# One-hot products for all 128 expert columns in one matmul each, placed beside the tiles of u

## What is computed

```python
q = (xb @ w_q).reshape(PEER_BLOCK, PEER_HEADS, 2, PEER_HALF)
scores = jnp.einsum('thpd,hpkd->thpk', q, sub_keys).astype(jnp.float32)
top_s, top_i = lax.top_k(scores, PEER_TOPK)
...
cand_i = (top_i[:, :, 0, :, None] * PEER_N_KEYS + top_i[:, :, 1, None, :]).reshape(...)
best_s, best_pos = lax.top_k(cand_s, PEER_TOPK)
expert = jnp.take_along_axis(cand_i, best_pos, axis=-1)
gate = jax.nn.softmax(best_s, axis=-1)
act = jax.nn.gelu(jnp.einsum('thkd,td->thk', u[expert], xb).astype(jnp.float32), approximate=False)
return jnp.einsum('thk,thkd->td', (gate * act).astype(v.dtype), v[expert])
```

## Time and profile before

| | us |
|---|---|
| median of 3 runs | 2359.57 (2357.17 to 2361.6) |
| the profiled execution, its own time | 2366.52 |
| its span, first to last instruction | 2365.1 |
| PE busy | 2232.4 (94%) |
| PEld busy | 1941.9 (82%) |
| DVE busy | 1621.3 (69%) |
| ACT busy | 1100.3 (47%) |
| POOL busy | 353.3 (15%) |
| share of the 16 DMA engines for loads | 44.8% |

### The profile page before, as it was taken

The page is one execution under the profiler, slowest core; times in us unless marked ns, Lnnn a source line. Parts: engine busy times, 40 slices in busy tenths (PEclk is TensorE's granted clock), DMA queues, the critical chain, the costliest instruction groups (busy, mean ns, idle before and its releaser), DMA issues.

```text
span 2365.1 us, 35299 instructions
## 1 busy us (share of the span) xinstructions
PE 2232.4 (94%) x14036; PEld 1941.9 (82%) x14036; DVE 1621.3 (69%) x2749; ACT 1100.3 (47%) x1671; POOL 353.3 (15%) x166
## 2 busy tenths in 40 slices
PE   8998979899999999799998878999999999999999
PEld 6887769888878887578887667999999998887887
DVE  5667793476666666866666765798466768897554
ACT  5554632155555555555555854444433333333443
POOL 0000102200010000100013112232222222222222
PEclk9998995799999999699999878999999999999999
DMA  5665130046545665146554224444544434443554
GB/s 193 189 191 173 61 134 11 1 153 190 190 162 178 189 189 171 45 136 191 189 198 161 80 81 160 164 163 159 182 148 150 144 127 147 149 146 128 187 194 153
DMA packets 96658, 352.15 MB, mean 149 GB/s; under 512 B 10880, under 2 KB 11776, under 8 KB 96048
## 3 DMA queue, kind: packets, MB, share of 16 engines
q1 hardware_dynamic: 96496, 349.90, 44.8%
HBM read 348.81 MB, written 1.05 MB: 148 GB/s over the span
## 4 chain that ended last, share of the span: by engine, by line
PE 80%; DVE 14%; ACT 3%; issue 1%; POOL 1%; DMA 0%; SPq 0%; ACTq 0%; DVEq 0%
PE psum L235 16%; PE psum L236 16%; PE psum L237 16%; PE psum L276 14%; PE psum L275 6%; PE psum L2494 4%; DVE tile_low L185 3%; PE psum L992 2%; ACT tile_high L173 1%; PE psum L279 1%; PE psum L318 1%; POOL small L1593 1%; DVE hT L468 1%; PE psum L756 1%; DVE peer_active L2696 1%
## 5 line engine op out<-in xcount | busy, mean ns | idle before, releaser
L173 ACT ACTIVATE tile_high<-raw_tiles 128x1024 fp32r<-128x1024 f32 x650 | 686.2, 1056 | 573.4 <-PE psum L237 573.1
L185 DVE TENSOR_TENSOR tile_low<-raw_tiles,tile_high 128x1024 fp32r<-128x1024 f32 x543 | 674.7, 1245 | 391.7 <-ACT tile_high L173 385.2
L276 PE MATMUL psum<-hT,tile_high 128*128 128x512 f32 x1408 | 495.2, 396 | 5.8 <-issue 5.2
L197 POOL TENSOR_TENSOR tile_low<-raw_tiles,tile_high 128x1024 fp32r<-128x1024 f32 x107 | 270.2, 2525 | 831.3 <-ACT tile_high L173 831.3
L235 PE MATMUL psum<-hT,tile_high 128*128 128x256 f32 x1280 | 372.5, 291 | 8.0 <-DVE tile_low L185 3.9
L235 PE MATMUL psum<-tile_high,hT 128*128 128x512 f32 (+1 forms) x848 | 346.4, 409 | 21.1 <-DVE mix_arena L2330 7.6
L236 PE MATMUL psum<-hT,tile_high 128*128 128x256 f32 x1280 | 365.5, 286 | 0.0
L237 PE MATMUL psum<-hT,tile_low 128*128 128x256 f32 x1280 | 365.3, 285 | 0.0
L275 PE MATMUL psum<-hT,tile_low 128*128 128x256 f32 x1232 | 344.3, 279 | 0.0
L236 PE MATMUL psum<-tile_low,hT 128*128 128x512 f32 (+1 forms) x848 | 335.8, 396 | 0.0
L237 PE MATMUL psum<-tile_high,hT 128*128 128x512 f32 (+1 forms) x848 | 335.4, 396 | 0.0
(11 more groups left out here) (332 smaller groups left out, 2790.8 us busy)
## 6 DMA issues: line engine op xcount, KB each, us to landing
raw_tiles<-ffn_in_dram SPq DMA_DIRECT2D x176, 512.0 KB, 3.8
raw_tiles<-peer_u_dram SPq DMA_DIRECT2D x128, 512.0 KB, 3.5
raw_tiles<-peer_v_dram SPq DMA_DIRECT2D x128, 512.0 KB, 3.5
raw_tiles<-ffn_out_dram SPq DMA_DIRECT2D x88, 512.0 KB, 3.5
raw_tiles<-w_kv_dram SPq DMA_DIRECT2D x16, 512.0 KB, 3.5
raw_tiles<-in_gates_dram SPq DMA_DIRECT2D x16, 512.0 KB, 3.5
raw_tiles<-peer_q_dram SPq DMA_DIRECT2D x16, 512.0 KB, 4.2
raw_tiles<-w_k_dram SPq DMA_DIRECT2D x8, 512.0 KB, 4.3
```

What stands on the lines that cost most here:

```text
L173: scalar.activation(k.high[:, n % SLOTS, :], k.raw[:, n % RAW_SLOTS, :], ACT.Copy).then_inc(*k.tile_high_made.mark(n))
L185: vector.tensor_tensor(k.low[:, n % SLOTS, :], k.raw[:, n % RAW_SLOTS, :], k.high[:, n % SLOTS, :].bitcast(F32), ALU.subtract).then_inc(*k ...
L197: pool.tensor_tensor(k.low[:, n % SLOTS, :], k.raw[:, n % RAW_SLOTS, :], k.high[:, n % SLOTS, :].bitcast(F32), ALU.subtract).then_inc(*k.p ...
L276: ins = k.tensor.matmul(ps, high[:, c, :], both[:, c, :, :], start=(c == 0), stop=(c == KC - 1), skip_group_check=True)
```

## The change

There is one side instead of two. `j_hot` and `j_gates` have all 128 columns, a lot's matmuls have 128 moving columns, and there are 64 lots in all. They stand after steps 68 to 131, beside tiles of u; none stand beside v.

When lot q is weighed (step 69 + q on VectorE), only the first `active_by(q)` columns of `active` exist: 52 for lot 0, 116 for lot 63. `weigh(q)` multiplies these in place. For the later columns the weights themselves are kept: `keep(q)`, new, on ScalarE one step later, copies them from PSUM to the place in `active` where the products will stand. When such a later column's tile is done, gelu is written in place into PSUM for the tokens whose weights wait (`waiting(g)` tokens) and into `active` for the rest, and `weigh_pair(g)`, new, on VectorE, multiplies the waiting weights by it. A lot's PSUM bank is emptied by `keep`, a pair's by `weigh_pair`.

At the turn from u to v, TensorE's sums in `hT` may be overwritten as soon as the last tile of u has passed those chunks (`chunks_passed`). At the end x takes in each of the four banks as soon as that bank is summed.

`j_hot` has a buffer of its own, single, and `hots(q)` waits for `hots(q - 1)`. The diff, cut to its core:

```diff
-FIRST_WEIGHED = len(range(0, 16)) + HALF + 1
+FIRST_WEIGHED = PICKS_AT + 2 * PICK_STEPS - 1
+def weighed_at(q):
+    return FIRST_WEIGHED + 3 + q
+def active_by(q):
+    return (weighed_at(q) - 2 * PH) // 2 * 2
+def waiting(g):
+    return LOT * sum(active_by(q) <= 2 * g for q in range(LOTS))
...
 # tensor_peer
-    def lot(side, q):
-        ps = bank(k, ("lot", side, q), k.weighed, (side, q))[:, 0:LOT * HALF].rearrange("p (j t) -> p j t", t=LOT)
+    def lot(q):
+        ps = bank(k, ("lot", q), k.weights_kept, q).rearrange("p (j t) -> p j t", t=LOT)
...
+    def chunks_passed(c, ins):
+        if c in (1, 3, 5):
+            ins.then_inc(*k.bank_summed.mark(("chunks", c // 2)))
...
-    while step < FIRST_WEIGHED + LOTS + 3:
-        beside(step)
-        step += 1
-    use_banks(k, range(4, 8))
...
-        if pair == HALF // 2:
-            while step < SECOND_WEIGHED + LOTS + 3:
-                beside(step)
-                step += 1
...
+                    if pair == PAIRS - 1 and i == 1 and (tb, half) != (1, 1):
+                        ins.then_inc(*k.bank_summed.mark(("peer", tb, half)))
             ins.then_inc(*k.tile_used.mark(n))
-            if pair < HALF // 2:
-                beside(step)
-                step += 1
...
 # scalar_peer
-            scalar.activation(r["active"][:, 2 * g:2 * g + 2, :], result(k, ("peer_u", g)).rearrange(
-                "p (j t) -> p j t", j=2), ACT.Gelu).then_inc(*k.activated.mark(g))
+            ps, n = result(k, ("peer_u", g)).rearrange("p (j t) -> p j t", j=2), waiting(g)
+            if n:
+                ins = scalar.activation(ps[:, :, 0:n], ps[:, :, 0:n], ACT.Gelu)
+            if n < T:
+                ins = scalar.activation(r["active"][:, 2 * g:2 * g + 2, n:T], ps[:, :, n:T], ACT.Gelu)
+            ins.then_inc(*k.activated.mark(("pair", g)))
+    def keep(q):
+        scalar.wait_ge(*k.weighed.at(q))
+        scalar.activation(r["active"][:, active_by(q):KEYS, lot_of(q)], result(k, ("lot", q)).rearrange(
+            "p (j t) -> p j t", t=LOT)[:, active_by(q):KEYS, :], ACT.Copy).then_inc(*k.weights_kept.mark(q))
...
     def part_high(pair):
         if pair >= 3:
             scalar.wait_ge(*k.tile_used.at(v + 2 * (pair - 3) + 1))
+        else:
+            scalar.wait_ge(*k.bank_summed.at(("chunks", pair)))
...
     for step in range(16 + KEYS):
+        if 0 <= step - 1 - weighed_at(0) < LOTS:
+            keep(step - 1 - weighed_at(0))
         if step and step % 2 == 0:
             out(step // 2 - 1)
         split_high(k, base + step + SLOTS)
         beside(step)
...
 # vector_peer
+        vector.tensor_tensor(j_hot, r["numbers"], across(r["j_of"](q), KEYS), ALU.is_equal).then_inc(*k.hot_steps.mark())
+        vector.tensor_tensor(i_hot, r["numbers"], across(r["i_of"](q), KEYS), ALU.is_equal).then_inc(*k.i_hot_made.mark(q))
         vector.wait_ge(*k.hot_steps.now())
+        vector.tensor_tensor(j_gates, j_hot.unsqueeze(1).to_broadcast([P, PARTS, KEYS, LOT]),
+                             r["gates_of"](q).unsqueeze(2).to_broadcast([P, PARTS, KEYS, LOT]), ALU.mult).then_inc(
+                                 *k.hot_made.mark(q))
...
+    def weigh_pair(g):
+        n = waiting(g)
+        if n:
+            a = r["active"][:, 2 * g:2 * g + 2, 0:n]
+            vector.wait_ge(*k.activated.at(("pair", g)))
+            vector.tensor_tensor(a, result(k, ("peer_u", g)).rearrange("p (j t) -> p j t", j=2)[:, :, 0:n], a,
+                                 ALU.mult).then_inc(*k.weighed.mark(("pair", g)))
...
+        if step % 2 == 0 and step >= 18:
+            weigh_pair(step // 2 - 9)
+        if 0 <= step - weighed_at(0) < LOTS:
+            weigh(step - weighed_at(0))
+        if 0 <= step - FIRST_WEIGHED - 1 < LOTS:
+            hots(step - FIRST_WEIGHED - 1)
...
-    vector.wait_ge(*k.tile_used.at(N_TILES - 1))
     for tb in range(TB):
         for half in range(2):
             xs = k.x[:, tb, half_of(half)]
-            vector.tensor_tensor(xs, k.psum[:, 2 * tb + half, :], xs, ALU.add).then_inc(*k.x_updated.mark(("peer", tb, half)))
+            vector.wait_ge(*(k.tile_used.at(N_TILES - 1) if (tb, half) == (1, 1) else k.bank_summed.at(("peer", tb, half))))
+            vector.tensor_tensor(xs, result(k, ("values", tb, half)), xs, ALU.add).then_inc(
+                *k.x_updated.mark(("peer", tb, half)))
```

More of the change, by code:

```diff
@@ L252, in half_of, with feature_major @@
     return slice(n * BANK, (n + 1) * BANK)
[L255 removed]
+def feature_major(k, ps, src, ready=None, passed=None):
     n, pair = take(k)
@@ L2517, in tensor_peer @@
             step += 1
-    for g in range(HALF):
-        ps = bank(k, ("peer_u", g), k.activated, g)
+    for g in range(PAIRS):
+        ps = bank(k, ("peer_u", g), k.weighed if waiting(g) else k.activated, ("pair", g))
         for i in range(2):
-            feature_major(k, ps[:, i * T:(i + 1) * T], k.hT)
+            feature_major(k, ps[:, i * T:(i + 1) * T], k.hT, passed=chunks_passed if (g, i) == (PAIRS - 1, 1) else None)
             beside(step)
             step += 1
-    while step < FIRST_WEIGHED + LOTS + 3:
-        beside(step)
-        step += 1
-    use_banks(k, range(4, 8))
[L2528 to L2531, removed]
-        if pair == HALF // 2:
-            while step < SECOND_WEIGHED + LOTS + 3:
-                beside(step)
-                step += 1
+    for tb in range(TB):
+        for half in range(2):
+            bank(k, ("values", tb, half), k.x_updated, ("peer", tb, half))
+    for pair in range(PAIRS):
         for i in range(2):
@@ L2607, in scalar_peer @@
         beside(step)
-    out(PH + HALF - 1)
-    step = 16 + KEYS
-    while step < FIRST_WEIGHED + LOTS + 3:
-        beside(step)
-        step += 1
-    part_high(0)
-    for pair in range(HALF):
-        if pair + 1 == HALF // 2:
-            while step < SECOND_WEIGHED + LOTS + 3:
-                beside(step)
-                step += 1
-        if pair + 1 < HALF:
+    part_high(0)
+    out(PH + PAIRS - 1)
+    for pair in range(PAIRS):
+        if pair + 1 < PAIRS:
             part_high(pair + 1)
@@ L2622, in scalar_peer @@
             split_high(k, v + 2 * pair + i + SLOTS)
-            if pair + 1 < HALF // 2:
-                beside(step)
-                step += 1
 def vector_peer(k):
@@ L2782, in vector_peer @@
         beside(step)
-    step = 16 + KEYS
-    while step < FIRST_WEIGHED + LOTS + 3:
-        beside(step)
-        step += 1
     part_low(0)
-    for pair in range(HALF):
-        if pair + 1 == HALF // 2:
-            while step < SECOND_WEIGHED + LOTS + 3:
-                beside(step)
-                step += 1
-        if pair + 1 < HALF:
+    weigh_pair(PAIRS - 1)
+    for pair in range(PAIRS):
+        if pair + 1 < PAIRS:
             part_low(pair + 1)
```

94 lines of the change are left out of this document (39 added, 55 removed).

## The result

| | before, us | after, us |
|---|---|---|
| median of 4 runs | 2360.6 (2357.2 to 2365.5) | 2332.0 (2329.2 to 2339.3) |
| the profiled execution's span | 2365.1 | 2328.5 |

The changed kernel takes 0.9883 of the time (95% interval 0.986 to 0.9906), 28.6 us less. 2294.5 was forecast, with a range of 2288 to 2318: the direction is right, the gain is less than half, and the time lies outside the range.

What follows compares the result with a forecast made beforehand. The prediction took TensorE to bound the expert stage; 3.2 + 0.6 − 6.5 − 61.0 − 2.6 − 1.8 + 3 = −65.1 us takes the profiled 2366.5 to 2301.4, a median of 2294.5, range 2288 to 2318.

Steps and rivals of the forecast that it cites:

- Part 1: Lots beside u: four more lots there cost +3.2 us, and doubling each lot's columns +0.6 us in all.
- The bound for added columns: Lots beside u: columns paid in full at 0.42 ns each, a lot of 1.11 us, +20 us in all.
- Rival C: Lots: operands four bf16 apart halve column reading; 111 ns a matmul, 1.36 us a lot, +36, 2331 us; chance 0.05.
- Rival A: Lots beside u: added columns cost time, 1.11 us a lot, 2314 us; chance 0.2.
- the 0.97 in its brackets: Lots: the Trainium skill's about 81 ns a matmul gives 0.97 us a lot, 2305 us.
- Rival D: Beside u: VectorE so late that TensorE stops every third tile, half clock follows; slower, 2379 us; chance 0.03.
- D's 4.1 us in three steps: Beside u: the time lost in three steps that gives +87 on 2291.5, 2379 us.
- Rival B: Beside u: VectorE becomes the bound, 0.3 us more a step than TensorE, +19 instead of +3, 2311 us; chance 0.2.
- Part 2: Turn from u to v: TensorE's 6.8 us gap shrinks to a wait of 0.3, −6.5 us.
- Part 3: V: all 128 tiles run as the second half did; −61.0 us in the first half, −2.6 in the second.
- Part 4: The end: three of four adds hide beside the next bank's matmuls, −1.8 us.
- Part 5: VectorE beside u: 9.8 to 11.1 us against TensorE's 11.0 in three steps; waits cost +3 us, bounds 0 and 19.

Runs made afterwards that it cites:

- the packed old form: Kernel before, its 128 narrow lots unmoved, each matmul's 64 moving and 64 output columns side by side; result not computed: 2322.4 us, 0.9837 of before.
- the token-by-token run: Changed kernel computing everything, j_hot, j_gates and PSUM bank laid out as (token, column), so moving and output columns are packed: 2362.8 us, 1.001 of before.
- the run with the turn undone: Changed kernel, but first three high parts wait for u's whole last tile and all four final adds for v's last: 672.1 us from last transposed pick against 668.9.

## Why the prediction was wrong

**Part 1 failed, and it alone made the miss.** The step that failed is its term for the 64 added columns: it said that a weight load sets the pace of a matmul, so that doubling the columns costs +0.6 us in all. It put a wide lot, with what it adds to a step, at 0.80 us; it takes 1.42. 64 × 0.62 is 39.7 us, so the term is 40 us and not 0.6; 2294.5 + 39.7 less the 3 us of waits that didn't come is 2331.2, and 2332.0 was measured. Two things in it were wrong:

- It took the f32 rows (L992 and L2476) as the nearest. They are near in having a weight load for each matmul, but they take 111 ns for 128 columns, twice as long as the columns themselves, so a stream at half rate would not show in them. The narrow lot was another case: it is held by its strided streams, and the packed old form shows 33 ns where the prediction saw a weight load of 63.
- The bound for added columns, 0.42 ns each, came from v's and u's matmuls, whose columns are packed in both streams. A bound must come from rows with the same access pattern; 64 more columns at half rate are 53 ns more a matmul, and 55 came.

**Rival C was the right one** for half of its reason, with a chance of 0.05: the step halves the rate at which columns are read. The output's step was in no rival, and C's narrow lots "at the pace of the weight load" are refuted by the 33 ns. That its price of 2331 is so near is partly luck: it took 111 ns from the f32 rows where 117 were measured, and kept 3 us of waits that didn't come. The numbers at hand could have spoken for C: 64 columns at half rate are 53 ns, and the row said 63. But a floor of 63 ns a matmul fitted the same row, and only a run could tell them apart. Rival A didn't come, neither with 1.11 us a lot nor with the 0.97 in its brackets: a lot is 1.42 strided and 0.70 packed.

Two sums of the rivals are a little off. 0.97 us is a lot by itself, and what it adds to a step is 0.03 more, as in the other sums; that makes 2307 and not 2305. D's 4.1 us in three steps leave B's 0.9 out; with it they are 5.0, and its price is 2398. Neither touches the forecast.

**Part 2 was right.** TensorE waits 0.29 us at the turn, with no half clock behind it (start us, us; idle before and its releaser):

```profile
1976.05 0.28 PE L237 MATMUL psum<-hT,tile_low 128*128 128x256 f32 x1
1976.62 0.47 PE L235 MATMUL psum<-tile_high,hT 128*128 128x512 f32 x1 [0.29 <-DVE hT L2795]
```

**Part 3 was right.** High parts in v are 2.72 us apart; the 348.4 us for 128 tiles were forecast as 348.2:

```profile
2202.76 1.06 ACT L173 ACTIVATE tile_high<-raw_tiles 128x1024 fp32r<-128x1024 f32 x1 [1.66 <-PE psum L237]
...
2205.48 1.06 ACT L173 ACTIVATE tile_high<-raw_tiles 128x1024 fp32r<-128x1024 f32 x1 [1.14 <-PE psum L237]
```

**Part 4 was right:** −1.8 forecast, 1.9 by the single execution of the run that undoes it.

**Part 5** sized VectorE's work rightly and its effect too high: +3 us was put for waits beside the lots, and none came. The changed kernel is no test of it, since its steps are 4.30 us long. The run with moving and output columns packed is, with the same work on VectorE in steps of 3.63 us: VectorE is busy 212.8 of 223 us, 95%, or 10.4 of the 10.9 us of three steps where 9.8 to 11.1 of 11.0 were put, and TensorE waits for nothing there. Rival B didn't come; its mechanism is real, but in the token-by-token run it took 0.8 us more for `j_gates`, 0.3 for `j_hot` and 0.4 for `weigh`. Rival D's half clock is not borne out for stops as long as those of that run: 62 stops of 1 us each, the longest 1.7, did not take the granted clock from 1.00, nor did the one of 1.5 us in the run with the turn undone. Stops of 2.5 us, as D has them, were not made. In the kernel before, TensorE idled 0.9, 0.4 and 2.0 us within some 5 us at the turn, and 0.9 and 3.4 us ahead of v's tile 64, and half clock followed both times (a granted clock of 0.86 from 1948 to 1960, and of 0.85 from 2183 to 2200). All its waits from 1942 on:

```profile
PE psum L235 <- DVE tile_low L185: 3.4, 1, 3.4
PE psum L2494 <- DVE peer_onehot L2740: 2.2, 3, 0.9
PE psum L235 <- DVE hT L2777: 2.0, 1, 2.0
```

**Where the 28 us came from.** Before, 60 lots stood beside u, 4 at the turn, 61 each behind a tile of v, and lots 61 to 63 of side 1 together between v's tiles 63 and 64. (So one lot each stands behind 61 tiles of v and not behind 62, as the text on the change has it.) With 0.86 us for 62 of those beside v and 0.79 for the other 66, the lots' time fell from about 105 us to 64 × 1.42 = 91, some 14 to 15 us. The rest is idle time, half clock and the end: 3.3 us idle at the turn, 0.3 of which are left, 4.3 ahead of v's tile 64, some 4 of half clock behind these two, 1.9 at the end. In this kernel's layout halving the number of lots is worth little by itself: 0.76 us for 64 columns against 1.42 for 128.

## What to carry to other kernels

Look at the step of both streams of a matmul, what it reads as moving operand and what it writes to PSUM, before pricing its columns: here either step halved the rate, and removing one of the two gave next to nothing (a lot of 1.34 or 1.42 us in place of 1.42). Where a layout suits the engine that writes it and not the one that reads it, try the smallest run that keeps the writer's rate; for VectorE's `j_gates` that was two bf16. And see whether the engine that reads PSUM can take the step in place of the matmul that writes it; here `weigh` did, with a step of 512 bytes, at no price. And take a bound from rows that share the access pattern, not only the shape; a row whose duration is near its columns at half rate is a hint that a stride is being paid, to be settled by a run that packs it.

## What the runs showed of the hardware

- A bf16 matmul of 128 columns with its own weight load: 56 ns from start to start packed, 59 with a moving step of two, 117 with one of four (output packed), 108 to 109 with an output step of two or of four f32. Of 64 columns: 33 ns packed, 62 with both steps four.
- A bf16 matmul of 64 columns and the weight load of 128 columns that goes with it take 33 ns together; the weights stood four bf16 apart there. Packing the weights alone took 2 ns of 117.
- VectorE, `j_gates` of 1536 bf16 elements: 947 ns with runs of four, 1746 with an operand that stands still in the innermost dimension. Of 768: 549 with runs of four, 547 with runs of two.
- VectorE's `weigh`: 493 to 504 ns on average with runs of four in SBUF and PSUM, 503 with a PSUM read step of 512 bytes, 877 with an SBUF inner step of 1 KB.
- Stops of TensorE of 1 us in each step of 4.70 us, 62 in a row, left the granted clock at 1.00.
